# One decoder layer on one core: unit 7 of the first weights ahead of the keys' norm, and the second query heads' sums, norm and split ahead of the biases of block 0's first two groups

## The reference

```
u   = rmsnorm(h, mix_norm_g)
qkv = u @ wqkv                    # 16 query heads, 4 key/value heads of 64
q   = rmsnorm(q per head, gq);  k = rmsnorm(k per head, gk)
s   = q.k / 8 - slope(head)*distance, for 0 <= distance < 128, else -inf
m   = max(max s, sink);  e = exp(s - m)
o   = (e / (sum e + exp(sink - m))) @ v
h   = h + o @ wo
h   = h + square(relu(rmsnorm(h) @ w1)) @ w2
out = h + sigmoid(rmsnorm(h) @ w_gate) * (p @ ple_w_proj)
```

## Time and profile before

| | |
|---|---|
| median of 3 runs | 1082.31 us (1082.21 to 1082.42) |
| the profiled execution | 1081.98 us |
| its span, first to last instruction | 1080.2 us |
| TensorE matmul busy | 1066.9 us, 99% |
| VectorE, ScalarE, GpSimd busy | 72%, 44%, 14% |
| granted TensorE clock | 1.00 |

### The profile page before, as it was taken

One profiled execution on the slowest core, in us unless ns is written; L12 is line 12 of the kernel. 1 busy time (PEld: TensorE's weight loads), 2 busy tenths in 40 slices (PEclk: granted clock), 3 DMA queues, 4 the chain that ended last, 5 costly groups with the idle time before them and its releaser, 6 DMA issues.

```text
span 1080.2 us, 14531 instructions
## 1 busy us (share of the span) xinstructions
PE 1066.9 (99%) x5014; PEld 884.4 (82%) x5014; DVE 779.6 (72%) x1147; ACT 477.7 (44%) x841; POOL 148.7 (14%) x271
## 2 busy tenths in 40 slices
PE   8999999999999999999999999999999999999998
PEld 6788888887888888888888888888888888888887
DVE  7877877778354599776677668376776878747985
ACT  7566666667323233413322342353333335427451
POOL 7544445443000000000000000000000000001000
PEclk9999999999999999999999999999999999999999
DMA  7000000050332325353343254998988898660102
GB/s 273 21 21 19 19 19 25 15 195 20 117 118 78 117 78 200 132 196 121 148 179 149 85 194 177 389 413 280 285 291 289 294 329 310 215 234 1 39 30 88
DMA packets 67232, 167.49 MB, mean 155 GB/s; under 512 B 5088, under 2 KB 6376, under 8 KB 67176
## 3 DMA queue, kind: packets, MB, share of 16 engines
q1 hardware_dynamic: 67152, 166.75, 42.9%
q10 hardware_dynamic: 24, 0.01, 0.0%
HBM read 128.99 MB, written 37.75 MB: 154 GB/s over the span
## 4 chain that ended last, share of the span: by engine, by line
PE 88%; DVE 7%; issue 2%; ACT 2%; POOL 1%; DMA 1%; SPq 0%; ACTq 0%; DVEq 0%; POOLq 0%
PE pair L2566 28%; PE pair L2546 22%; PE pair L2269 10%; PE pair L2413 8%; PE pair L2612 6%; PE pair L2504 3%; PE pair L2340 3%; PE pair L2308 2%; PE pair L2639 2%; PE pair L2474 1%; PE pair L2319 1%; POOL k_rstd L790 1%; DMA RES<-in_a_wqkv 1%; PE pair L2234 0%; DVE RES L1944 0%
## 5 line engine op out<-in xcount | busy, mean ns | idle before, releaser
L2566 PE MATMUL pair<-uT 128*128 128x512 f32 x1344 | 305.9, 389 | 0.0
L2566 PEld LDWEIGHTS pair<-uT 128*128 128x128 f32 x1344 | 252.0, 188 | 52.5 <-DVE uT L1957 0.3
L1296 ACT ACTIVATE uT<-wo_raw 128x1024 fp32r<-128x1024 f32 x83 | 84.6, 1054 | 114.0 <-PE pair L2566 97.3
L1957 DVE TENSOR_TENSOR uT<-wo_raw,uT 128x1024 fp32r<-128x1024 f32 x83 | 98.6, 1222 | 45.8 <-ACT uT L1296 45.5
L772 POOL TENSOR_SCALAR row_var<-row_ssq 128x1 f32<-128x1 f32 x16 | 3.1, 195 | 708.7 <-ACT hn L1337 625.5
L2413 PE MATMUL pair<-WA,oT 128*128 128x512 f32 x384 | 90.3, 392 | 0.6 <-DVE oT L1720 0.4
L2269 PE MATMUL pair<-WA,xT 128*128 128x512 f32 x336 | 83.7, 397 | 1.2 <-DVE xT L1516 0.4
L2413 PEld LDWEIGHTS pair<-WA,oT 128*128 128x128 f32 x384 | 71.2, 188 | 15.9 <-issue 1.4
L2546 PE MATMUL pair<-WA,WB 128*128 128x512 f32 x336 | 78.2, 389 | 0.4 <-ACT xr L1271 0.4
L2546 PEld LDWEIGHTS pair<-WA,WB 128*128 128x128 f32 x336 | 63.0, 188 | 13.8 <-DVE WB L1891 0.8
L2269 PEld LDWEIGHTS pair<-WA,xT 128*128 128x128 f32 x336 | 60.9, 188 | 14.4 <-issue 2.3
(11 more groups left out here) (239 smaller groups left out, 1790.0 us busy)
## 6 DMA issues: line engine op xcount, KB each, us to landing
wo_raw<-in_m_w SPq DMA_DIRECT2D x71, 512.0 KB, 6.4
wo_raw<-hid_kept SPq DMA_DIRECT2D x41, 512.0 KB, 5.8
hid_kept<-RES SPq DMA_DIRECT2D x32, 512.0 KB, 2.7
emb<-in_m_w SPq DMA_DIRECT2D x17, 512.0 KB, 6.1
RES<-in_m_w SPq DMA_DIRECT2D x8, 1024.0 KB, 6.8
uT_f<-in_m_w SPq DMA_DIRECT2D x6, 1024.0 KB, 6.6
RES<-in_a_wqkv SPq DMA_DIRECT2D x10, 512.0 KB, 8.6
emb<-hid_kept SPq DMA_DIRECT2D x10, 512.0 KB, 5.8
```

Of the source, the lines that this page charges most:

```text
L1296: nc.scalar.activation(operand(t, which, HI), unit(t, which), ACT.Copy).then_inc(op_hi, 1)
L1957: nc.vector.tensor_tensor(operand(t, which, LO), unit(t, which), operand(t, which, HI).bitcast(F32), ALU.subtract).then_inc(op_ready, 1)
L2566: mm = nc.tensor.matmul(ps[4 * (j % 2) + m][:], operand(t, 0, s)[:, k, m * P:(m + 1) * P], operand(t, 1, r)[:, k, :], start=(g == 0 and k ...
```

## The change

Four edits, in the opening stage and block 0 only:

- VectorE splits unit 7 ahead of the keys' head_scale, and TensorE does the two matmuls (LO,3) of q0 ahead of turn_k(0).
- VectorE's nsink (the negated sinks) moves from ahead of unit 11 to the end of the opening stage.
- In j = 0 of block 0 VectorE does the head sums of q8 ahead of the bias of group 0, and head_scale of q8 and v_diff ahead of invert and scale of group 0. In j = 1 it does q_lo_part of q8 ahead of the bias of group 1.
- ScalarE's x_squares(1) moves from behind exps(0,0) to behind q_hi_part of q8, ahead of exps(0,1).

```diff
@@ ScalarE, body @@
                     if j == 1:
                         q_hi_part("q8", n, 0)
                         q_hi_part("q8", n, 1)
+                        if first:
+                            x_squares(n + 1)
...
-                    if j == 0 and not last:
+                    if j == 0 and not first and not last:
                         x_squares(n + 1)
@@ VectorE, body @@
                     if j == 0 and first:
                         xT_lo_half(1, 0)
                         xT_lo_half(1, 1)
+                        head_sums("q8", n)
                         add_bias(n, j, first)
-                        head_sums("q8", n)
+                        head_scale("q8", n)
+                        v_diff(n)
                         invert(n, j)
                         scale_probs(n, j)
-                        head_scale("q8", n)
-                        v_diff(n)
                         continue
+                    if j == 1 and first:
+                        q_lo_part("q8", n, 0)
+                        q_lo_part("q8", n, 1)
...
-                    if j == 1:
+                    if j == 1 and not first:
                         q_lo_part("q8", n, 0)
                         q_lo_part("q8", n, 1)
@@ VectorE, opening stage @@
             lo_unit(6, "q0", 2)
+            lo_unit(7, "q0", 3)
             head_scale("k", 0)
-            lo_unit(7, "q0", 3)
             lo_unit(8, "q8", 0)
...
             head_scale("q0", 0)
-            dve.wait_ge(consts_in, 16)
-            nc.vector.tensor_scalar(nsink[:], sink[:], -1.0, None, ALU.mult)
             lo_unit(11, "q8", 3)
             q_lo_part("q0", 0, 0)
             q_lo_part("q0", 0, 1)
+            dve.wait_ge(consts_in, 16)
+            nc.vector.tensor_scalar(nsink[:], sink[:], -1.0, None, ALU.mult)
             body(0, first=True)
@@ TensorE, opening stage @@
-            project_first("q0", (HI, 0), (HI, 1), (LO, 0), (LO, 1), (HI, 2), (HI, 3), (LO, 2))
+            project_first("q0", (HI, 0), (HI, 1), (LO, 0), (LO, 1), (HI, 2), (HI, 3), (LO, 2), (LO, 3))
             turn_k(0)
-            project_first("q0", (LO, 3))
             project_first("q8", (HI, 0), (HI, 1), (LO, 0), (HI, 2), (LO, 1))
```

## The result

The changed kernel takes 1084.2 us (median of 20 runs, 1083.65 to 1084.56), the kernel before 1082.24 us (20 runs beside it, 1081.59 to 1082.58): ratio 1.0018, 95% interval [1.0012, 1.0024], 1.96 us slower. Forecast were 1084.3 and +2.03 us. The profiled execution took 1084.22 us, its span is 1082.5 us.

A forecast was written before the change was run, and what follows sets the result against it. TensorE, busy 99%, was taken as the bound. The front's -0.51 us is spent before scores(0,1); the split's +0.82 at scores(0,2) becomes +2.03 at the projection through GpSimd, giving a median of 1084.3 us, range 1083.0 to 1085.1.

The forecast's parts named there:

- The front: Opening stage: unit 7 and two matmuls moved ahead bring q0's squares and what follows 0.51 us earlier, spent before scores(0,1).
- The unknown price of the front: Opening stage: VectorE's split of unit 7 may hold GpSimd's k_rstd, from no loss to no gain; no loss taken.
- my lower bound: Opening stage: k_rstd gets in between units 6 and 7 on the shared port, so the front loses nothing.
- The second rival: Opening stage: k_rstd waits for both halves of unit 7, later steps 0.5 more: +2.5 us, 1084.8; chance 0.12.
- Head sums first: Block 0, j = 0: group 0's bias starts 0.10 us later, scores(0,1) at 33.37, turn_q at 36.63; 0.17 us gained there.
- The split ahead of the bias: Block 0, j = 1: VectorE idles some 2 us, group 1's bias starts at 39.49, scores(0,2) at 41.22, +0.82 us.
- GpSimd: Block 1's keys' norm: q_var moves to 44.42, k_var to 50.09 behind bias rows, the projection to 52.37: +2.03 us.
- the first rival: Projection of q8: GpSimd does not hold the keys' norm, or the wait is partly absorbed: +0.8 us, 1083.1; chance 0.11.
- The third rival: Scores(0,2): the split does not hold the bias up, scores at 39.89, needing turn_q 1.3 us earlier: 1081.8; chance 0.05.
- The clock: TensorE: idle gaps of about 1.3 us leave the granted clock at 1.00, so nothing was charged for it.

The follow-up runs named there:

- e1: The kernel before with only the opening-stage edits (unit 7, the two matmuls, nsink): ratio 0.9997, median -0.32 us against the kernel before.
- e2: The kernel before with only q8's head sums, norm and v_diff moved ahead in j = 0: ratio 0.9996, median -0.40 us against the kernel before.
- e4: The changed kernel with GpSimd's norm of block 1's keys ahead of group 2's bias rows: ratio 1.0010, median +0.89 us against the kernel before.
- e8: The changed kernel with turn_q(q8) three matmuls behind scores(0,1) instead of nine: ratio 1.0006, median +0.53 us against the kernel before.
- e5: The changed kernel with q8's split back behind group 1's bias and x_squares(1) back behind exps(0,0): ratio 0.9994, median -0.64 us against the kernel before.
- e9: e5 with turn_q(q8) three matmuls behind scores(0,1) and three q0 matmuls ahead of scores(0,1): ratio 0.9991, median -1.07 us against the kernel before.

## Why the prediction was right

It was right in time (1084.3 for 1084.2) and in mechanism, and its main terms were each seen alone.

- The front. Forecast -0.51, for scores(0,0) as for all behind it; measured 29.95 - 0.30 - 30.11 = -0.46 in the changed kernel, and -0.41 at the projection in e1. The norm of the keys stood back to back with unit 7 and in time for turn_k, at 20.97. Right, 0.05 to 0.1 too large. Moving nsink cost nothing: VectorE's next row, at 30.18, follows ScalarE's half by 0.63 us, where it was 0.64 before.
- The unknown price of the front. k_rstd took 1.42 us beside the split of unit 7 (1.41 before, rows 4): it was not held for a half of unit 7, my lower bound. The second rival falls for this kernel. VectorE was not held either: its six halves of units 5 to 7, 0.75 us each, ran in 4.23 us, 0.70 from start to start, and the last two, from about 18.4 on, lie beside k_rstd (17.80 to 19.22). By the rule of the Trainium skill (SBUF — State Buffer, "Who interferes with whom"), whoever comes first holds the port for its whole instruction; then either k_rstd should have taken longer or the split from 18.4 should have waited for its end. The trace shows neither. No run measured the exclusion by itself, so why k_rstd got in, and what its 1.41 us are made of, is open.
- Head sums first. scores(0,1) forecast at 33.37, measured 33.71 - 0.30 = 33.41; turn_q 36.63 and 36.51. The gain of the front is lost in 0.53 us of wait, as predicted. e2 shows that this term is no loss: VectorE comes to group 1's bias 0.52 us sooner by it. The changed kernel can't use that, since there VectorE stands idle ahead of the split.
- The split ahead of the bias. scores(0,2) forecast at 41.22, measured 41.17; idle 1.53. That it fits to 0.05 is in part luck: the split ended at 39.69 - 0.30 = 39.39, 0.16 sooner than worked out, and the bias started 0.04 behind its end, where I had it start 0.07 ahead of it.
- GpSimd. q_var forecast at 44.42, measured 44.35; k_var 50.09 and 50.05; the projection 52.37 and 52.29. e4 shows that this is the term I said, and the first rival (only TensorE's own delay stays, +0.8) describes e4, not the changed kernel.
- The third rival named the right threshold at the scores: from 1.3 us earlier on the wait should go, and at 1.34 us earlier (e8) 0.18 us was left, scores(0,2) less the offset at 39.83 where I had put 39.89. It missed that the time would not follow: I had priced it at -0.5 by that gate alone, where GpSimd's queue makes it +0.5 to +0.6.
- The clock. With gaps of 1.53 and 1.27 us the granted clock stayed at 1.00, the upper of its two levels, in both stretches (40 to 44 and 50 to 54 us).

What was off: e2 and e5 came out about 0.2 us better at scores(0,2) (39.92 for 40.1, 39.46 for 39.6) and at the projection than worked out, since one length was too large: I had turn_q 3.26 us behind scores(0,1), the start of before less the idle time in its bracket (36.80 - 0.27 - 33.27). Where it does not wait, it follows after 3.10 us (36.81 - 33.71). Idle time is counted from the modelled end of the matmuls ahead, and in the changed kernel the turn starts 0.16 us before that end (34.74 + 2.23 = 36.97). In e2 and e5 that let the turn, and with it ScalarE's half of the split and exps(0,1), come sooner than worked out.

## What to carry to other kernels

On an in-order queue, an instruction moved ahead is worth nothing until its last input is there: read when the input comes from the queue of the engine that makes it (here turn_q, which nothing had made earlier), and take what stands behind it as delayed until then. A delay is followed on every engine that hangs on the one behind: 0.8 us at TensorE's next gate became 2.0 us at the one after, through a third engine with 0.44 us of slack. And where an order is undone, undo what it hid too: the square of x was free in the changed kernel and cost 1 us in the same place once the wait around it was gone.

## What the runs showed that was not expected

The opening stage, before any edited instruction, is not the same length in every execution, and this is about as large as the smaller effects here. The eight transposes of x that start near 4.6 us took 1.39 us in the profile of before, 1.94 us in that of the changed kernel and 1.20 us in e9; the matmuls at 15.92 came up to 0.38 us later. TensorE of the changed kernel and then of e9:

```profile
4.57 1.94 PE L2239 MATMUL pair<-ident,xb 128*128 128x128 f32 x8
```

```profile
4.49 1.20 PE L2234 MATMUL pair<-ident,xb 128*128 128x128 f32 x8
```

The two do not go together one to one (e9 was 0.24 late all the same; there ScalarE waited 0.40 us for a transfer of weights at 8.23, which it did not before), and what lengthens the transposes stays open. The stretch from the projection to the end is not the same in every execution either: 1029.8 to 1030.3 us in the twelve profiles, though hardly any edit reaches into it. It matters for reading: a trace is aligned on a row ahead of the first edit before its gates are compared, and an effect of 0.3 us isn't taken from one span.
